# Rounding block 1's input projection into three passes, and giving the two branches of the last attention opposite halves of the array's rows

## The reference

```python
# block 1
mod = silu(c) @ w_ada + b_ada                 # six vectors of 1024
hmix = rmsnorm(x, w) * (1.0 + scale1) + shift1
proj = hmix @ w_in                            # 512 x 1024 @ 1024 x 3600
cb, cc, cx, nq, nk, nv, gqkv, gz, ga, gb = split(proj)   # ga, gb: 8 columns each, gates
y_conv = cb * dwconv(cc * cx)                 # then attention, a gated delta scan, experts
# block 3, the last attention
s1 = q1 @ k1.T / 8;  s2 = q2 @ k2.T / 8       # 8 heads, 64 features each, causal
att = (softmax(s1) - lam * softmax(s2)) @ v   # swept in blocks of 128 queries
```

## Time and profile before

| | us |
|---|---|
| median of three runs (3404.41 to 3411.51) | 3406.36 |
| the profiled execution's own time | 3404.7 |
| its span, first to last instruction | 3402.9 |
| PE busy, of the span | 3078.0 (90%) |
| DVE busy | 1617.6 (48%) |
| ACT busy | 1021.7 (30%) |
| mean granted TensorE clock, of full | 0.938 |

### The profile page before, as it was taken

How to read it: one execution, slowest core, us unless ns; L and a number is a source line. 1 busy time by engine, 2 the same in 40 slices (tenths; PEclk the granted TensorE clock), 3 DMA queues, 4 the chain that set the end, 5 groups by cost and what they waited for, 6 DMA issues and landing times.

```text
span 3402.9 us, 36376 instructions
## 1 busy us (share of the span) xinstructions
PE 3078.0 (90%) x14824; PEld 2134.2 (63%) x14824; DVE 1617.6 (48%) x2634; ACT 1021.7 (30%) x1634; POOL 21.2 (1%) x40
## 2 busy tenths in 40 slices
PE   7998798698898979999999799989899979879998
PEld 3544786444344457787647578876677756658776
DVE  5334753323223244233834345544698957443343
ACT  2216223201001042262442422233322255342343
POOL 0000000000000000000000000000000000000000
PEclk9898989699999988899999899999899989989999
DMA  8340000699999942121031145431122210032220
GB/s 307 133 148 1 3 1 6 271 427 428 427 428 427 387 164 75 50 99 50 26 121 65 56 149 198 173 136 50 50 84 96 85 39 25 25 136 90 96 75 25
DMA packets 140187, 479.10 MB, mean 141 GB/s; under 512 B 7440, under 2 KB 11152, under 8 KB 125968
## 3 DMA queue, kind: packets, MB, share of 16 engines
q1 hardware_dynamic: 131696, 459.55, 35.2%
q10 hardware_dynamic: 5760, 8.14, 0.7%
q0 software_dynamic: 2592, 9.44, 0.7%
HBM read 472.92 MB, written 4.19 MB: 140 GB/s over the span
## 4 chain that ended last, share of the span: by engine, by line
PE 72%; DMA 12%; DVE 10%; ACT 4%; issue 2%; SPq 1%; ACTq 0%; DVEq 0%; POOLq 0%; POOL 0%
PE bank L457 14%; PE bank L459 14%; PE bank L458 14%; DMA ring<-in_expert_w 9%; PE bank L356 5%; PE bank L1739 5%; PE bank L2283 3%; PE bank L578 2%; DVE A L2894 2%; DMA A<-in_expert_w 1%; PE bank L1229 1%; DVE ring_parts L453 1%; PE bank L2957 1%; PE bank L2080 1%; PE bank L2079 1%
## 5 line engine op out<-in xcount | busy, mean ns | idle before, releaser
L458 PE MATMUL bank<-h_parts,A_parts 128*128 128x512 f32 x896 | 352.8, 394 | 0.0
L459 PE MATMUL bank<-h_parts,ring_parts 128*128 128x512 f32 x880 | 346.6, 394 | 0.0
L457 PE MATMUL bank<-h_parts,A_parts 128*128 128x512 f32 x800 | 316.3, 395 | 23.0 <-DVE ring_parts L453 12.9
L453 DVE TENSOR_TENSOR ring_parts<-ring,A_parts 128x1024 fp32r<-128x1024 f32 x178 | 217.6, 1224 | 242.0 <-ACT A_parts L446 242.0
L446 ACT ACTIVATE A_parts<-ring 128x1024 fp32r<-128x1024 f32 x178 | 187.3, 1053 | 462.7 <-PE bank L459 443.5
L1739 PE MATMUL bank<-ring,A 128*64 128x512 f32 x864 | 268.2, 629 | 36.0 <-DMA ring<-in_expert_w 25.6
L459 PE MATMUL bank<-A_parts,ring_parts 128*128 128x512 f32 x608 | 239.5, 394 | 0.0
L457 PE MATMUL bank<-A_parts 128*128 128x512 f32 x528 | 211.7, 401 | 4.0 <-DVE ring_parts L453 3.8
L1739 PEld LDWEIGHTS bank<-ring,A 128*64 128x64 f32 x864 | 88.9, 144 | 200.8 <-issue 199.2
L458 PE MATMUL bank<-ring_parts 128*128 128x512 f32 x528 | 208.2, 394 | 0.0
L458 PEld LDWEIGHTS bank<-h_parts,A_parts 128*128 128x128 f32 x896 | 170.9, 191 | 36.0 <-issue 0.7
(11 more groups left out here) (546 smaller groups left out, 5471.0 us busy)
## 6 DMA issues: line engine op xcount, KB each, us to landing
ring<-in_expert_w SPq DMA_DIRECT2D x72, 2048.0 KB, 17.7
ring<-in_w_in SPq DMA_DIRECT2D x37, 2048.0 KB, 8.1
A<-in_expert_w SPq DMA_DIRECT2D x36, 2048.0 KB, 21.3
ring<-in_w_ada SPq DMA_DIRECT2D x24, 2048.0 KB, 12.5
ring<-in_w_ff SPq DMA_DIRECT2D x16, 2048.0 KB, 8.1
ring<-in_w_ffn_gate SPq DMA_DIRECT2D x5, 2048.0 KB, 7.9
ring<-in_w_ffn_up SPq DMA_DIRECT2D x5, 2048.0 KB, 7.9
ring<-in_w_o SPq DMA_DIRECT2D x4, 2048.0 KB, 7.7
```

The lines of the kernel that those rows point to most:

```text
L453: eng.tensor_tensor(parts(s.raw()), s.raw(), parts(s.shaped(high(s.q % 2))), ALU.subtract)\
L457: pe.matmul(out, parts(w_high), parts(r_low), start=start, stop=False)
L458: pe.matmul(out, parts(w_high), parts(r_high), start=False, stop=False)
L459: return pe.matmul(out, parts(w_low), parts(r_high), start=False, stop=stop)
```

## The change

Three edits, and the numbers that they need:

1. Every matmul of the input projection becomes three passes of rounded parts. ACT writes h rounded (`in_x_high`), DVE the rest (`in_low`); each slice of `w_in` is split by ACT and DVE two tiles ahead (`split_next`). The 16 gate columns become the weights and h the moving operand, giving 16x512, which is turned back by four transposes. The values keep h as weights (256 columns of the moving operand). The first two tiles use `project_begin`.
2. The sums of `w_ada` on DVE (`ada_sum`) are spread, two instructions for each tile, among the splits; the masks' additions (`bias_dve`) too, one for each tile. Each is now added up by PE behind the piece of the projection that runs meanwhile. The ring's slots of this stretch are set by hand (slot 3 holds rounded slices from `cc_in` on), and ada7 is loaded behind `kv_in`.
3. In the last attention the second branch of each head is laid in the other 64 partitions (the host swaps the two heads of each pair in the columns of q2 and k2), and `scores` takes its rows from there.

```diff
-        summed(f"ada{4 + ada}", w["w_ada"], 4 + ada)
+        if name != "ab_in":
+            summed(f"ada{4 + ada}", w["w_ada"], 4 + ada)
+    summed(f"ada{4 + ada}", w["w_ada"], 4 + ada)
...
+    in_slots = {layers[name][0]: s for name, s in (
+        ("ab_in", 2), ("kv_in", 3), ("ada7", 2), ("xq_in", 1), ("ada8", 0), ("cc_in", 2), ("ada9", 0), ("z_in", 1),
+        ("ada10", 0), ("ada11", 2), ("out", 0))}
     for i, g in enumerate(order):
+        slot = in_slots.get(g, slot)
...
+            if begin:
+                begin()
...
+        in_x_high = lambda k: W(28 + k)
+        early_high = lambda slot: A[:, 2 * slot:2 * slot + 2, :].rearrange("p a n -> p (a n)")
+        late_high = lambda slot: ring[:, 3, 2 * T * slot:2 * T * (slot + 1)]
+        v_high = lambda slot: A[:, 24 + 2 * slot:26 + 2 * slot, :].rearrange("p a n -> p (a n)")
+        ab_high = A[:, 46, P:2 * P].rearrange("p (k n) -> p k n", k=KD)
+        ab_rows = A[0:16, 4, :]
...
+                return ring_tile(self.g)[:, self.k0:self.k0 + 4, 256:512]
...
+        for m, s in enumerate(kv_slices):
+            s.free = ("tile_ready", kv.first_tile + m + 1)
+        for i, s in enumerate(in_slices):
+            s.before = in_slices[i - 2] if i >= 2 else None
+        XQ_AT = len(gdn_slices) + len(kv_slices)
+        in_high = lambda i: early_high if i < XQ_AT + 4 else late_high
...
         def in_pe(pe):
-            for i in range(3):
-                project(pe, L[f"gdn_in{i}"], Hn,
-                        first=(lambda k: pe.wait_ge(*norm_at("n1", "out", k + 1))) if i == 0 else None)
+            project_begin(pe, gdn_slices[:2], early_high, in_x_high, Hn, lambda k: norm_at("n1", "out", k + 1),
+                          lambda k: pe.wait_ge(sem("in_low"), k + 1))
+            project_split(pe, gdn_slices[2:4], early_high, in_x_high, Hn)
+            sum_pe(pe, L["ada4"][0])
...
+            pe.wait_ge(sem("ab_low"), 1)
             bank_free(pe, g.first_tile)
+            for k in range(KD):
+                mm = three_passes(pe, bank[g.first_tile % 4][0:16, :], ab_high[:, k, :], ring_tile(g)[:, k, :],
+                                  in_x_high(k), Hn(k), k == 0, k == KD - 1)
+            mm.then_inc(sem("tile_ready"), 1)
+            project_split(pe, kv_slices[:1], early_high, in_x_high, Hn)
+            pe.wait_ge(sem("tile_read"), g.first_tile + 1)
             for t in range(TT):
-                for k in range(KD):
-                    mm = pe.matmul(bank[g.first_tile % 4][:, 16 * t:16 * t + 16], Hn(k)[:, t * P:(t + 1) * P],
-                                   ring_tile(g)[:, k, :], start=(k == 0), stop=(k == KD - 1))
-            mm.then_inc(sem("tile_ready"), 1)
-            sum_pe(pe, L["ada7"][0])
-            g = L["kv_in"][0]
-            for m in range(2):
-                tile = g.first_tile + m
-                weights_here(pe, g)
+                mm = pe.transpose(bank[6][:, 16 * t:16 * t + 16], ab_rows[:, t * P:(t + 1) * P],
+                                  sq("ident")[0:16, 0:16])
+            mm.then_inc(sem("ab_turned"), 1)
+            project_split(pe, kv_slices[1:], early_high, in_x_high, Hn)
+            for t in range(TT):
+                tile, c = kv.first_tile + 2 + t, slice(t * P, (t + 1) * P)
                 bank_free(pe, tile)
                 for k in range(KD):
-                    mm = pe.matmul(bank[tile % 4][:], ring_tile(g)[:, k, m * P:(m + 1) * P], Hn(k),
-                                   start=(k == 0), stop=(k == KD - 1))
+                    s = value_slices[k // 4]
+                    pe.wait_ge(sem("split_low"), s.q + 1)
+                    mm = three_passes(pe, bank[tile % 4][:, 0:256], in_x_high(k)[:, c], Hn(k)[:, c],
+                                      s.shaped(v_high(s.q % 2))[:, k % 4, :], s.raw()[:, k % 4, :],
+                                      k == 0, k == KD - 1)
                 mm.then_inc(sem("tile_ready"), 1)
-            project_tokens(pe, g, lambda k, t: Hn(k)[:, t * P:(t + 1) * P], 256, 256, g.first_tile + 2)
+            sum_pe(pe, L["ada7"][0])
             gdn_gates_pe(pe)
-            for i, name in enumerate(("xq_in", "cc_in", "z_in")):
-                sum_pe(pe, L[f"ada{8 + i}"][0])
-                project(pe, L[name], Hn)
+            project_split(pe, xq_slices, early_high, in_x_high, Hn)
+            sum_pe(pe, L["ada8"][0])
+            project_split(pe, cc_slices, late_high, in_x_high, Hn)
+            sum_pe(pe, L["ada9"][0])
+            project_split(pe, z_slices, late_high, in_x_high, Hn)
+            sum_pe(pe, L["ada10"][0])
...
+        def in_begin_act(act):
+            for s in gdn_slices[:2]:
+                split_high(act, s, early_high)
...
+            def split_next(i):
+                if i + 2 < len(in_slices):
+                    split_high(act, in_slices[i + 2], in_high(i + 2))
+            ab_in = L["ab_in"][0]
             for j, tile in enumerate(gdn_tiles):
+                split_next(j)
...
+            for s in value_slices:
+                split_high(act, s, v_high)
             silu(11)
-            b = read_tile(act, L["ab_in"][0].first_tile)
-            act.activation(small[:, 16:80], b[:, 0:64], ACT.Copy).then_inc(sem("tile_read"), 1)
+            b = read_tile(act, ab_in.first_tile)
+            act.activation(ab_rows, b[0:16, :], ACT.Copy).then_inc(sem("tile_read"), 1)
+            b = read_tile(act, kv.first_tile)
+            act.activation(W(8), b[:], ACT.Copy).then_inc(sem("tile_read"), 1)
+            split_next(12)
+            act.wait_ge(sem("ab_turned"), 1)
+            act.activation(small[:, 16:80], bank[6][:, 0:64], ACT.Copy).then_inc(sem("ab_here"), 1)
+            gdn_softplus_act(act)
+            split_next(13)
+            b = read_tile(act, kv.first_tile + 1)
+            act.activation(W(9), b[:], ACT.Copy).then_inc(sem("tile_read"), 1)
...
+        def in_begin_dve(dve):
+            for s in gdn_slices[:2]:
+                split_low(dve, s, early_high)
+        def in_low(dve, k):
+            dve.wait_ge(*norm_at("n1", "out", k + 1))
+            dve.scalar_tensor_tensor(parts(Hn(k)), Hn(k), mod[:, k:k + 1], parts(in_x_high(k)), ALU.add,
+                                     ALU.subtract).then_inc(sem("in_low"), 1)
         def in_dve(dve):
             step = ordered(dve, "conv_dve")
             cond = small[:, 4:12]
+            def split_next(i):
+                if i + 2 < len(in_slices):
+                    split_low(dve, in_slices[i + 2], in_high(i + 2))
             for j, tile in enumerate(gdn_tiles):
-                if j % 4 == 0:
-                    ada_sum(dve, L[f"ada{4 + j // 4}"][0], cond, step)
+                ada_sum(dve, L[f"ada{4 + j // 4}"][0], cond, step, range(2 * (j % 4), 2 * (j % 4) + 2))
+                split_next(j)
+                if j == 9:
+                    dve.wait_ge(sem("ab_high"), 1)
+                    t = ring_tile(L["ab_in"][0])
+                    dve.tensor_tensor(parts(t), t, parts(ab_high), ALU.subtract).then_inc(sem("ab_low"), 1)
                 dve.wait_ge(sem("tile_read"), tile + 1)
                 if j >= 2:
                     dve.wait_ge(*seen("gdn_silu", j - 1))
                 conv3(dve, step, W(44 + j % 2), W(12 + j),
                       lambda i, j=j: col("gdn_conv_w", 12 * i + j)).then_inc(signal("gdn_conved"), 1)
+            for s in value_slices:
+                split_low(dve, s, v_high)
             ada_sum(dve, L["ada7"][0], cond, step)
+            split_next(12)
             gdn_gates_dve(dve)
-            ada_sum(dve, L["ada8"][0], cond, step)
-            gdn_decays_dve(dve)
-            bias_dve(dve)
-            for i in range(9, 11):
-                ada_sum(dve, L[f"ada{i}"][0], cond, step)
+            split_next(13)
+            for i, g in enumerate((L["ada8"][0], L["ada9"][0])):
+                for m in range(4):
+                    ada_sum(dve, g, cond, step, range(2 * m, 2 * m + 2))
+                    split_next(XQ_AT + 4 * i + m)
+                    if i == 0 and m == 0:
+                        gdn_decays_dve(dve)
+                    bias_dve(dve, i, m)
             dve.wait_ge(*seen("gdn_silu", 12))
-            dve.wait_ge(sem("tile_read"), L["cc_in"][0].first_tile + 4)
             for j in range(2):
+                split_next(XQ_AT + 8 + j)
+                dve.wait_ge(sem("tile_read"), L["cc_in"][0].first_tile + 4)
                 step(dve.tensor_tensor(W(2 + j), W(2 + j), W(4 + j), ALU.mult))
                 step(conv3(dve, step, W(44), W(2 + j), lambda i, j=j: col("conv_a_w", 2 * i + j)))
                 then(dve.tensor_tensor(W(j), W(j), W(44), ALU.mult), "y_conv")
                 dve.wait_ge(*seen("y_conv", j + 1))
+            ada_sum(dve, L["ada10"][0], cond, step)
...
             def scores(u):
                 q, i = dunits[u]
-                r, n = 64 * (i % 2), P * (q + 1)
+                n = P * (q + 1)
                 if u >= 2:
```

(7 more changed lines are left out.)

58 lines of the change are left out of this document (35 added, 23 removed).

## The result

The changed kernel takes **3374.05 us** (median of 5, 3372.12 to 3385.08), the kernel before 3405.24 beside it: ratio 0.9912, 95% interval 0.9894 to 0.9930. The forecast was 3376, range 3364 to 3389. So the number came out within 2 us, but by luck, as the sum of two errors of opposite sign: the projection with the neighbourhood attention behind it gave 20.0 us where the sum had 24.8, and the last attention gave 10.0 where it had 5.5.

What follows compares the result with a forecast made beforehand. PE was taken to bound the kernel, busy for 90% of the span. From 3404.7 us, the projection's terms took 24.8 and the last attention 5.5, giving 3374.4, or 3376 against the median; range 3364 to 3389.

Steps and rivals of the forecast that it cites:

- The tile, 5.44: Input projection: a tile in three passes takes 5.44 us against 6.89, saving 1.45; the skill's figure would give 5.17.
- The first two tiles, +5.5: Start of the projection: DVE's pace replaces PE's, so the third tile starts at 66.0 us and 5.5 us are lost.
- Ten gdn tiles and their sums, -12.0: Projection: ten further gdn tiles save 14.5 us, and PE's waits for sums at each fourth tile cost 2.5.
- Gates, keys, values, and the wait behind them, -8.4: Projection: these tiles save 15.4 us; a wait for the second key tile's bank costs 4.0, half clock behind it 3.0.
- xq, cc, z, -17.4: Projection: twelve tiles of xq, cc and z save 17.4 us, with DVE's 3.8 us per tile under PE's 5.44.
- The end, +7.5 to the first scores: End of the projection: PE stands 6.0 us for DVE's last work and loses 1.5 to a lowered clock.
- the attention starts cold, +1.5: Start of the neighbourhood attention: PE's clock is down after the pause, costing 0.93 us for first scores, the rest for tiny sums.
- four slots become three: Last attention: score records on opposite row halves partly overlap, 8.6 us less on PE, of which 5.5 on the path.
- Rival 1: The pauses don't come (-7 us) or the last attention gains in full (-7 more): 3362 to 3369; chance 0.14.
- Rival 2: Value passes slower (+7), row halves don't overlap (+5.5), gates at half clock (+5); one or two: 3381 to 3389; chance 0.16.
- Rival 3: Slower: PE's clock falls to half for over 60 us of the projection, a loss of 30 us; chance 0.03.
- Rival 4: No change: DVE or its loads bind the projection's tiles, 6.7 us a turn for 4.75, about 3402; chance 0.03.

Runs made afterwards that it cites:

- begin_both: Changed kernel, with PE making the high-part passes of the first two gdn tiles for both tiles at each k: 3366.7 us, ratio 0.9900 to the kernel before.
- sums_late: Changed kernel, with the last two sums of w_ada moved from ahead of the neighbourhood attention to within it: 3368.6 us, ratio 0.9887 to the kernel before.
- gates_moving: Changed kernel, with the gates' roles turned back (tokens as weights, 16 gate columns moving, three passes, no transposes): 3386.1 us, ratio 0.9955 to the kernel before.
- all_four: Changed kernel plus early second-key-tile copy, last w_ada sums within the attention, both first tiles at each k, sum steps as 4, 2, 2, 0: 3357.4 us, 0.9859.
- three_of_four: Changed kernel plus early second-key-tile copy, last w_ada sums within the attention, both first tiles at each k; sum steps stay 2, 2, 2, 2: 3360.0 us, 0.9866.

## Why the number was right and two of its steps were not

- **The tile, 5.44**: as predicted, from 70 to 230 us, and not the 5.17 set against it; only the first tile behind a sum took 5.6.
- **The first two tiles, +5.5**: the third starts at 65.9 for a predicted 66.0. `begin_both` shows that the order of the passes, and not DVE's pace alone, made this loss: with another order 4.4 us of it went at the first tile, and 2.5 were left at M.
- **Ten gdn tiles and their sums, -12.0**: -10.6. The waits were 1.6, 0.5 and 0.5, near the forecast (1.8, 0.4, 0.3). The sums' own records took 1.05 where I had 0.79, and the first tile behind a sum 5.6 for 5.44, so the gates begin at 126.6 for 125.3 by these terms.
- **Gates, keys, values, and the wait behind them, -8.4**: 46.05 us (131.84 to 177.89) became 36.5 (126.58 to 163.03), -9.6. The wait was 4.0, as forecast; the fourth value tile behind it took 4.65 for 2.9, and little else ran at half clock. The gates at 5.6 and the value tiles at 2.88 were near the lower ends of their bounds.
- **xq, cc, z, -17.4**: -17.0.
- **The end, +7.5 to the first scores**: +8.0, of which PE's waits for the last two sums are 6.0, as forecast.
- **What failed: "the attention starts cold, +1.5".** The term was mis-sized: it ended at the first scores. PE stayed at half clock to 256 us, and from the scores to M it lost another 3.7 us (70.3 for 66.6). `sums_late` shows that not all of it comes from the wait ahead, so how much of the 3.7 is this wait's stays open. With some 1 us net of the lines above, the 24.8 became 20.0.
- **What failed: "four slots become three".** The step took it that records start in program order, branch by branch. They start in twos, and the slots are two: 1.91 became 1.06 a unit, and 10.0 us were on the path for 5.5. Rival 1 had two slots in it at 7 us more; they came at 4.5. The Trainium skill's TensorEngine Tiling (Array Packing), section Theoretical Speedup, gives up to 2x for a contraction of 64; the trace has 1.8x at 512 columns and 1.7x at 384 (busy time, above), and agrees. I had set against it TensorE: Matmul & The Clock Gate, Part 3, by which matmuls stay in program order and only the weights' loads are pulled ahead. The rows don't tell which branch each record of a pair belongs to, so they don't decide on that rule; what they refute is the slot count that I drew from it.

Rival 2 (narrow passes, no overlap, gates at half clock) failed in all three parts; `gates_moving` shows that with the old roles its third part would have come true, at 12 us and not 5. Rival 3, the clock, was seen in small: some 11 us in the first tiles (47 to 58), some 4 behind the values' wait, 21 at the attention's start, never 60. Rival 4 (DVE binds) may have been nearer than its 0.03 says: with a pass left out the group still took 22.5 to 23.1 us under PE's 23.4, though part of that was half clock.

Open: why the clock falls at the start of the neighbourhood attention when no wait for sums stands ahead of it, why it falls behind the same work in one execution and not in another, and what decides how long it stays down in the scan.

## What to carry to other kernels

When a faster stage runs into the next one's start, price the half clock there up to where the rows are back at their full pace, not up to the first instruction: here that stretch cost 5 us and not 1.5, though part of it came without the wait too. An experiment that takes one wait away can show little, because half clock a few us on, or in a stretch that it doesn't touch, takes up the gain; compare a mark in the trace behind each stage, and try the edits together before dropping one. And two float32 matmuls with a contraction of 64 on opposite row halves, one behind the other, cost here about what one does: 1.06 us for 1.91 at 512 columns.

## What was not expected of the hardware

- **The granted clock in the delta scan differs from execution to execution of the same kernel.** M to N took 270.4 to 275.8 us in ten of the profiled executions and 286.4 to 288.6 in four. Behind N all agree to 1.4 us, the two without the halves apart, so this is nearly the whole difference between the changed kernel's two profiled executions, and larger than most edits tried here; that the unprofiled runs scatter for the same reason is not shown. The Trainium skill says in TensorE: Matmul & The Clock Gate, Part 1, that the number of cold matmuls varies from run to run of one kernel; the trace agrees, in the middle of a kernel and at 11.5 us between two executions.
- **Where PE was full, the clock came back sooner**: at 50.8 with both tiles at each k, at 58.1 with 0.46 us of gap at each k, from about the same start (47.3 and 47.5). In 46:58 the mean clock was 0.68 to 0.82 in the four kernels with both tiles at each k, and 0.50 in all eight executions with the old order on PE.
- **The same thin records cost the clock in one execution and not in another**: behind eight sum records and twelve of the gates, with PE's wait of 0.8 us ahead, it was 0.50 in `all_four` and 1.00 in `three_of_four`. So a fall behind such a place in one profile doesn't tell what an edit did.
